# RWKV-7 chunk stage: the block inverses of both head halves taken level by level in turn, ahead of all sums

## The chip, the cores and the metric

The kernel runs on one core of one Trainium2 chip. The metric is the device time of one execution in microseconds (us). Engines are named as in the profile: PE is TensorE's matmul side, PEld its weight loads, DVE is VectorE, ACT is ScalarE, POOL is GpSimd, SP is SyncE, which issues loads. Everything is float32; a float32 product shows as two PE records.

## The reference, cut to what matters

Two decoder layers are computed for 1,040 prompt tokens (16 meta tokens and 1,024 others) and for 8 samples of 4 tokens. Layer 0 mixes with latent attention, layer 1 with RWKV-7 time mixing, and each is followed by a squared-ReLU MLP. The change touches RWKV-7 alone, which has 16 heads of 64 and, by token,

```python
def _wkv_step(S, inp):
    r, w, k, v, a, b = inp
    sa = jnp.einsum('bhvk,bhk->bhv', S, a)
    S = S * w[:, :, None, :] + sa[..., None] * b[:, :, None, :] + v[..., None] * k[:, :, None, :]
    return S, jnp.einsum('bhvk,bhk->bhv', S, r)
```

Then `y` is normalized by head, scaled by `ln_w`, shifted by `ln_b`, gets the term `(sum(r*k*r_k)) * v`, is multiplied by a gate and goes through `w_o`.

## The kernel before

**Chunks.** The recurrence is done in chunks of 128 tokens: chunks 0 to 7 in `chunk(c, ...)`, and a tail of 48 tokens behind them. Chunks 1 to 6 run in a hardware loop of three turns with two chunks each. Inside a chunk the state solves a triangular system for each head, so a 128x128 unit triangular matrix is inverted by head. Heads are done in two halves of eight, d = 0 and d = 1.

**The inverse.** `low_inverses(c)` on DVE inverts the 16x16 diagonal blocks of all 16 heads of a chunk and signals `low_b` at its last transpose (line 2899). It needs `diagonals(c)` on ACT (line 2141), which copies the blocks out of the masked products `MA`, and those are made by `before_keys(c)` on PE and masked on DVE (line 2800). The larger blocks come from three levels, each a pair of dependent products with a copy behind each: `level_16` (spread block X4 from ACT line 2178, W4 masked on DVE line 2831, sum in `blocks_32`, lines 2836 and 2838, signalled by `e32_b`), `level_32` (X5 and XT spread by ACT line 2178, W5 by line 2197, XT by line 2203) and `level_64` (turned block, XW6 by ACT lines 1835 and 2211, XT by line 2215). X4, X5, W5 and XT each exist once, so the second half can begin only after the first is through.

**The sums.** `b_with_r`, `k_with_both` make products that DVE masks (line 2800). `first_sums(d)` gives P1; `finals(d)` multiplies P1 by the inverse, whose copy is `SA` (ACT line 1835), makes the change of the state (read by DVE's `new_half(d)`, lines 2946 and 2734) and the outputs Y.

**Preparing chunk c+1 inside chunk c.** Its path is: `key_sums` (PE), `clamp` (DVE line 2738), `norms` (ACT line 2124), `inverse_norms` (DVE line 2760), `key_scales` (PE), `normed_keys` (DVE line 2766); `rates` (PE), `both_rates` (ACT line 2109), `sums` (DVE lines 2751 to 2755, signals `cum_b`); `sums_before` (POOL line 1739), `decays_before` (ACT line 2134), `a_keys` (DVE line 2772), `b_keys` (DVE lines 2734 and 2782, signals `b_b`), `before_keys` (PE), `k_keys` (DVE), `diagonals` and `low_inverses`.

**Finishing chunk c-1 inside chunk c.** `centre` (DVE), `squares` (ACT line 2229), `variances` (DVE), `deviations` (ACT line 2233), `scale_outputs` (DVE lines 2923 and 2925, signals `scaled_b`), `group_norm` on POOL (lines 1744, 1746, 1748), `gates` (PE), `gated` (DVE line 2933), `turn_z` (PE), `z_to_store` (ACT).

**Order.** There is no planner. Each engine's `chunk` is a list written out by hand and each engine works through its own list in order; semaphores (`Beat.wait`) hold an engine until another has signalled. Two rings of four PSUM banks each lie between PE and ACT (`ra`) and between PE and DVE (`rv`). `keep_busy` is a product of 256 columns that nobody reads; a chunk has nine of them. POOL's list, which the change leaves alone, is:

```python
if prepare: scale_keys(c + 1, wn)
if finish:  y_b.wait(pool, c - 1); bonus_terms(c - 1, ...)
if finish:  group_norm(c - 1, P, Y[1 - par], vt[1 - par])   # waits scaled_b
if prepare: sums_before(c + 1, wn)                           # waits cum_b
...
if prepare: decay_r(c + 1, ...); bonus(c + 1, wn)
if finish:  store_z(c - 1)
```

`finish` is false in chunk 0 alone. PE's list before is b_with_r(0), k_with_both(0), level_16(0), level_32(0), level_64(0), finals(0), then b_with_r(1), k_with_both(1), level_16(1), before_keys(c+1), level_32(1), level_64(1), finals(1), with other work as fillers between the two products of each level.

Of the kernel before, what the change touches and what calls it, by code (L numbers as in the profile page):

```python
# [18 lines left out]
P = 128  # L19
# [141 lines left out]
def program(nc, A, O):  # L161
    ctx = ExitStack()
    with ctx:
# [180 lines left out]
        X4, X5, W5 = q(512), q(1024), q(1024)  # L344
# [10 lines left out]
        W4 = hx[:, 7168:8192]  # L355
# [25 lines left out]
        values_4 = [X5, W5]  # L381
# [80 lines left out]
        def _(pe):  # L462
# [532 lines left out]
            def turn_b_k(c, w):  # L995

                bk_b.wait(pe, c)
                for src in (Bt, Kt):
# [87 lines left out]
            def level_16(c, d, ma, filler):  # L1086
# [3 lines left out]
                for j in range(8):  # L1090
                    for rows, cols in diagonal(8 * d + j):
                        ins = mm(b[rows, j * 64:(j + 1) * 64], ma[rows, cols], X4[rows, j * 64:(j + 1) * 64], True, True)
                rv.done(ins)
                w4_at = rv.filled.n
                filler()
                if d == 1:
                    keep_busy(rv)
                b = narrow(rv, w4_at)
# [6 lines left out]
            def level_32(c, d, ma, filler):  # L1105
# [7 lines left out]
                w5_at = ra.filled.n  # L1113
                filler()
                xt_b.wait(pe, c, d + 1)
                keep_busy(ra)
                b = narrow(ra, w5_at)
                for j in range(8):
                    for rows, cols in diagonal(j):
                        ins = mm(b[rows, j * 64:(j + 1) * 64], W5[rows, j * 64:(j + 1) * 64], XT[rows, cols], True, True)  # L1120
                ra.done(ins)

            def level_64(d, ma, fillers):

                crossed_at = ra.filled.n
                fillers[2]()
                keep_busy(ra)
                b = narrow(ra, crossed_at)
                for j in range(8):
                    ins = turn(b[0:64, j * 64:(j + 1) * 64], XT[0:64, j * P:j * P + 64], 64)  # L1130
                ra.done(ins)
                turned_at = ra.filled.n
                fillers[0]()
                keep_busy(ra)
                b = narrow(ra, turned_at)
# [4 lines left out]
                w6_at = ra.filled.n  # L1140
                fillers[1]()
                b = narrow(ra, w6_at)
                for j in range(8):
                    ins = mm(b[0:64, j * 64:(j + 1) * 64], XW6[64:P, j * 64:(j + 1) * 64], XT[64:P, j * P + 64:(j + 1) * P], True, True)
                ra.done(ins)

            def chunk(c, par, nth, finish=True, prepare=True, wn=P):
# [15 lines left out]
                def finals(d, taken, stated):  # L1163
# [4 lines left out]
                    for j in range(8):  # L1168
                        ins = mm(b[:, j * RN:(j + 1) * RN], XT[:, j * P:(j + 1) * P],
# [45 lines left out]
                level_16(c, 1, ma, nothing)  # L1215
# [610 lines left out]
        def _(act):  # L1826
# [333 lines left out]
            def tokens(w):  # L2160
                for dst in (Btok, Ktok):
# [19 lines left out]
            def spread_16(c, d):  # L2181

                low_b.wait(act, c)
                if not isinstance(c, int) or c > 0 or d > 0:
                    e32_b.wait(act, c, d)
                signal(quadrants(X4, 64, XE[:, d * 256:(d + 1) * 256]), x4_b)

            def spread_32(c, d):

                e32_b.wait(act, c, d + 1)  # L2190
                signal(quadrants(X5[:, 0:512], 64, XE32), x5_b)
                signal(quadrants(XT, P, XD32), xt_b)

            def take_w_32():
                b = ring.bank()
                for rows in (32, 96):
                    ins = act.copy(heads(W5[:, 0:512], 64)[rows:rows + 32, :, 0:32], heads(b[:, :], 64)[rows:rows + 32, :, 0:32])
                lane.do(ins, ring.drained)

            def take_x_32():  # L2200
                b = ring.bank()
                for rows in (0, 64):
                    ins = act.copy(heads(XT, P)[rows:rows + 32, :, rows + 32:rows + 64], heads(b[:, :], 64)[rows:rows + 32, :, 32:64])
# [9 lines left out]
            def take_x_64():  # L2213
                b = ring.bank()
                lane.do(act.copy(heads(XT, P)[0:64, :, 64:P], heads(b[:, :], 64)[0:64, :, :]), ring.drained)
# [30 lines left out]
            def chunk(c, par, finish=True, prepare=True, wn=P):  # L2246
                if prepare:
                    lora_columns(c + 1, wn)
                tokens(P)
                spread_32(c, 0)  # L2250
                take_w_32()
                bonus_out(P)
                if prepare:
                    square_keys(c + 1, wn)
                take_x_32()
                bonus_factors(par, P)
                if finish:
# [12 lines left out]
                spread_16(c, 1)  # L2270
# [6 lines left out]

# [895 lines left out]
```

How the kernel before makes its waits and increments, by code:

```python
    def bank(self, free=False, ahead=0):  # L110
        n = self.filled.n + ahead
        if n >= len(self.banks) and not free:
            self.eng.wait_ge(self.drained, self.filled.value(len(self.banks) - 1 - ahead))
        return self.banks[n % len(self.banks)]
# [4 lines left out]
    def wait_drained(self, back=0):  # L120
        self.eng.wait_ge(self.drained, self.filled.value(back))
# [8 lines left out]
    def wait(self, eng, chunk, n=None):  # L131
        eng.wait_ge(self.sem, chunk * self.per + (self.per if n is None else n))
# [8 lines left out]
    def bank(self):  # L141
        self.eng.wait_ge(self.filled, self.drained.value(-1))
        return self.banks[self.drained.n % len(self.banks)]
# [12 lines left out]
    def settle(self):  # L157
        self.eng.wait_ge(self.last.sem, self.last.value())
# [289 lines left out]
        def meet(eng, here):  # L448
            here.add(eng.drain())
            here.n += 4
            eng.wait_ge(meet_s, here.n)
# [19 lines left out]
            def apart(semaphore, value):  # L472
                pe.wait_ge(semaphore, value)
                pe.sem_inc(narrow_s, 1)
# [4 lines left out]
            def norm(scratch, n):  # L480
                for at, w in PIECES:
                    sq_t.expect()
                    pe.wait_ge(sq_s, sq_t.n)
                    b = ra.bank()
                    for k in range(n):
                        ins = mm(b[:, 0:w], ones, scratch[:, k, at:at + w], k == 0, k == n - 1)
                    ra.done(ins)
# [1 line left out]
            def sums_at(layer, p, ks, b):  # L490
                w = PIECES[p][1]
                sq_t.expect()
                pe.wait_ge(sq_s, sq_t.n)
                for k in ks:
```

## Time and profile before

| what | value |
|---|---|
| three runs | 3689.3, 3693.97, 3695.07 us; median 3693.97 |
| profiled execution | 3694.62 us; span of its records 3692.9 us |
| PE busy in the span | 3481.3 us, 94% |
| DVE, ACT, POOL busy | 47%, 26%, 16% |
| mean granted TensorE clock | 0.959 of full |
| chunk stage (first to ninth `low_inverses`) | 2086.6 to 2676.4 us |

The profile gives one execution. The chunk stage is a sixth of it. The granted clock is the share of TensorE's full clock of 2.4 GHz that the chip allowed; it has two levels, 1.0 and 0.5 (2.4 and 1.2 GHz). A row of the timeline is: start in us, duration in us, engine, line, operation, output<-input, size, count, and in brackets how long the engine was idle before it and who ended that.

### The profile page before, as it was taken

What the parts mean: (1) busy time and instruction counts of PE and PEld (TensorE: products, weight loads), DVE (VectorE), ACT (ScalarE), POOL (GpSimd) and SP (SyncE); (2) the same over time, 40 slices, a digit from 0 to 9 for tenths busy, and PEclk for the clock granted to TensorE, in tenths of its full rate; (3) what the DMA queues carried; (4) which work ended last, traced back from release to release, by engine and by line L of the source; (5) the groups of instructions that cost most, each with busy time, mean ns of one, the idle gap of its engine ahead of it and who ended that gap; (6) DMA issues with size and microseconds to landing.
All of it is one profiled execution on the core that took longest, in us unless ns stands there. A gap on an engine that the chain in (4) does not pass through costs nothing.

```text
span 3692.9 us, 62858 instructions
## 1 busy us (share of the span) xinstructions
PE 3481.3 (94%) x24636; PEld 3069.2 (83%) x24636; DVE 1734.6 (47%) x3220; ACT 976.3 (26%) x1832; POOL 582.1 (16%) x241
## 2 busy tenths in 40 slices
PE   9999998999999999998999788888899999999998
PEld 6667666756999999996899677777785799999998
DVE  3545454214544444446203367667631644444445
ACT  2223333511111111112214255556520211111111
POOL 0000000000211212211222122223220122221111
PEclk9999998999999999999999889999969999999999
DMA  3222121510111111102222101000151111111101
GB/s 101 55 75 59 41 71 44 198 56 34 46 45 45 45 45 45 45 1 93 83 71 102 65 13 41 30 25 24 31 171 35 57 46 45 45 45 45 45 29 48
DMA packets 151723, 207.26 MB, mean 56 GB/s; under 512 B 42670, under 2 KB 126689, under 8 KB 151170
## 3 DMA queue, kind: packets, MB, share of 16 engines
q1 hardware_dynamic: 145506, 185.08, 15.2%
q0 software_dynamic: 6048, 19.73, 1.6%
q8 instruction: 130, 2.13, 0.2%
q14 instruction: 39, 0.32, 0.0%
HBM read 174.39 MB, written 50.82 MB: 61 GB/s over the span
## 4 chain that ended last, share of the span: by engine, by line
PE 66%; PEld 6%; DVE 5%; issue 3%; ACT 1%; DMA 1%; SPq 0%; DVEq 0%; ACTq 0%; PEldq 0%; POOLq 0%; POOL 0%
PE bank L470 64%; PEld bank L470 6%; PE bank L478 2%; DVE hT L2800 1%; DVE arena L2734 1%; DVE arena L2635 1%; SPq L1399 0%; ACT arena L2178 0%; DMA arena<-in_rwkv_a_w 0%; DVE n_lo L2602 0%; DVE arena L2751 0%; DMA arena<-arena 0%; ACT arena L1835 0%; DVE arena L2782 0%; DVE arena L2766 0%
## 5 line engine op out<-in xcount | busy, mean ns | idle before, releaser
L470 PE MATMUL bank<-arena 128*32 128x128 f32 (+15 forms) x8142 | 1174.2, 340 | 95.6 <-DVE hT L2800 26.5
L470 PEld LDWEIGHTS bank<-arena 128*128 128x128 f32 (+7 forms) x8142 | 837.5, 180 | 410.2 <-issue 122.1
L2433 DVE TENSOR_TENSOR hT<-hT,bank 128x384 f32<-128x384 f32 (+1 forms) x816 | 425.7, 526 | 501.9 <-PE bank L470 501.5
L470 PE MATMUL bank<-u_hi,dn_hi 128*128 128x384 f32 (+1 forms) x1536 | 494.9, 326 | 12.9 <-DVE hT L2433 8.3
L470 PE MATMUL bank<-u_lo,dn_hi 128*128 128x384 f32 (+1 forms) x1536 | 496.1, 327 | 0.0
L470 PE MATMUL bank<-n_hi,up_hi 128*128 128x384 f32 (+1 forms) x1536 | 489.6, 325 | 2.2 <-ACT arena L2019 2.2
L470 PE MATMUL bank<-n_lo,up_hi 128*128 128x384 f32 (+1 forms) x1536 | 489.5, 325 | 0.0
L1835 ACT COPY arena<-bank 128x512 f32<-128x512 f32 (+15 forms) x573 | 261.2, 491 | 856.5 <-PE bank L470 598.8
L1672 POOL TENSOR_TENSOR up_lo<-arena,up_hi 128x2048 fp32r<-128x2048 f32 x32 | 148.0, 4624 | 1559.9 <-ACT up_hi L2003 1559.9
L470 PE MATMUL bank<-u_hi,dn_lo 128*128 128x384 f32 (+1 forms) x1536 | 375.2, 326 | 0.0
L2635 DVE TENSOR_TENSOR arena<-arena 128x384 f32<-128x384 f32 (+1 forms) x192 | 163.9, 854 | 435.4 <-ACT arena L2019 435.4
L470 PEld LDWEIGHTS bank<-u_hi,dn_hi 128*128 128x128 f32 x1536 | 289.4, 188 | 15.4 <-DVE hT L2433 8.9
L470 PEld LDWEIGHTS bank<-n_hi,up_hi 128*128 128x128 f32 x1536 | 289.5, 188 | 2.9 <-ACT arena L2019 2.5
L470 PEld LDWEIGHTS bank<-u_lo,dn_hi 128*128 128x128 f32 x1536 | 289.8, 189 | 0.3
L470 PEld LDWEIGHTS bank<-n_lo,up_hi 128*128 128x128 f32 x1536 | 289.3, 188 | 0.1
L470 PE MATMUL bank<-n_hi,up_lo 128*128 128x384 f32 (+1 forms) x1536 | 282.4, 325 | 1.2 <-POOL up_lo L1672 1.2
L470 PEld LDWEIGHTS bank<-u_hi,dn_lo 128*128 128x128 f32 x1536 | 271.6, 189 | 0.0
L470 PEld LDWEIGHTS bank<-n_hi,up_lo 128*128 128x128 f32 x1536 | 256.1, 188 | 1.5 <-POOL up_lo L1672 1.5
L2019 ACT ACTIVATE arena<-bank 128x384 f32<-128x384 f32 (+1 forms) x192 | 89.6, 469 | 591.3 <-PE bank L470 584.2
L1672 POOL TENSOR_TENSOR dn_lo<-arena,dn_hi 128x2048 fp32r<-128x2048 f32 x32 | 147.4, 4606 | 617.5 <-ACT dn_hi L2009 617.5
L2009 ACT ACTIVATE dn_hi<-arena 128x2048 fp32r<-128x2048 f32 x32 | 61.4, 1920 | 649.9 <-PE bank L470 643.9
L470 PE MATMUL bank<-arena,hT 64*64 64x64 f32 (+3 forms) x2432 | 170.5, 255 | 47.1 <-ACT arena L2178 25.8
(207 smaller groups left out, 3948.6 us busy)
## 6 DMA issues: line engine op xcount, KB each, us to landing
arena<-in_ffn_w_up SPq DMA_DIRECT2D x32, 1024.0 KB, 5.6
arena<-in_ffn_w_down SPq DMA_DIRECT2D x32, 1024.0 KB, 7.7
arena<-past_scratch SPq DMA_DIRECT2D x32, 640.0 KB, 8.1
past_scratch<-in_cache_kv_latent SPq DMA_DIRECT2D x128, 128.0 KB, 2.4
hidden_scratch<-hT SPq DMA_DIRECT2D x1, 4288.0 KB, 13.1
past_scratch<-in_cache_k_rope SPq DMA_DIRECT2D x128, 32.0 KB, 2.1
arena<-in_rwkv_w_r SPq DMA_DIRECT2D x4, 1024.0 KB, 8.0
r_scratch<-arena POOLq DMA_DIRECT2D x8, 512.0 KB, 5.7
```

The lines of the kernel that those rows point to most:

```text
L470: return pe.matmul(out, lhsT, rhs, start=first, stop=last, skip_group_check=group)
L478: return pe.transpose(out, src, ident[0:rows, 0:rows])
L1672: lo_t.add(pool.tensor_tensor(lo[:, :, :], raw[:, :, :], hi[:, :, :].bitcast(F32), ALU.subtract))
L1835: lane.do(act.copy(dst, b if view is None else view(b)), ring.drained)
L2009: lane.do(act.activation(dn_hi[:, :, :], w_dn[par][:, :, :], ACT.Copy), hi_t)
L2019: lane.do(act.activation(relu[(u_t.n - 1) % 4][:, 0:w], b[:, 0:w], ACT.Relu), ring.drained)
L2433: lane.do(dve.tensor_tensor(hT[:, k, at:at + w], hT[:, k, at:at + w], b[:, 0:w], ALU.add), ring.drained)
L2635: lane.do(dve.tensor_tensor(r, r, r, ALU.mult))
L2734: lane.do(dve.tensor_tensor(out, a, b, op))
L2800: lane.do(dve.tensor_tensor(dst.rearrange("p (h z w) -> p h z w", h=heads, z=2)[:, :, z, :], b[:, 0:heads * n].rearrange("p (h w) -> p h w ...
```

## The change

X4 and XT get a second buffer each (X4 one by half, `XTs` one by half), each of the three level functions is cut into its first and second product, and PE's list in a chunk becomes: the levels of both halves step by step in turn, then the sums of half 0, then the sums of half 1, with `before_keys(c+1)` and `gates` and `turn_z` around the sums of half 1. ACT and DVE take their copies and masks in the matching order, and some other steps change places in their lists (`scale_outputs` behind `sums`, `norms` and `deviations` behind the SA copy, `diagonals` behind the second SA copy, both `spread_16` at the chunk's end). Nine `keep_busy` stay in a chunk; six of them now lie between the level steps. Four memsets at the stage's start become six (X4 twice, XT twice).

```diff
             def chunk(c, par, nth, finish=True, prepare=True, wn=P):    # PE
+                level_16_first(c, 0, ma)
                 r_b.wait(pe, c)
                 b_with_r(0, ar)
+                level_16_second(0)
+                level_16_first(c, 1, ma)
                 bk_b.wait(pe, c)
                 k_with_both(0, 0, ar)
                 k_with_both(0, 1, ar)
-                level_16(c, 0, ma, lambda: turn_b_k(c, P))
-                level_32(c, 0, ma, lambda: bonus_sums(c, P))
-                bonus_at = ra.filled.n - 1
+                level_16_second(1)
+                keep_busy(ra)
+                level_32_first(c, 0, ma)
+                turn_b_k(c, P, (Bt,))
+                keep_busy(ra)
+                level_32_second(c, 0)
+                bonus_sums(c, P)
+                bonus_at = ra.filled.n
+                level_32_first(c, 1, ma)
+                turn_b_k(c, P, (Kt,))
+                level_64_turned(0)
+                level_32_second(c, 1)
+                keep_busy(rv)
+                level_64_first(0, ma)
+                keep_busy(rv)
+                level_64_turned(1)
+                keep_busy(rv)
+                level_64_second(0)
+                keep_busy(rv)
+                level_64_first(1, ma)
                 v_in[par].wait(pe, nth)
-                level_64(0, ma, [when(prepare, lambda: key_sums(c + 1, wn)), lambda: first_sums(0), lambda: turn_bonus(P, bonus_at)])
+                first_sums(0)
+                if prepare:
+                    key_sums(c + 1, wn)
+                level_64_second(1)
+                turn_bonus(P, bonus_at)
                 finals(0, when(prepare, lambda: rates(c + 1, wn, 0)), when(prepare, lambda: (rates(c + 1, wn, 1), key_scales(c + 1, wn))))
 
                 b_with_r(1, ar)
                 k_with_both(1, 0, ar)
                 k_with_both(1, 1, ar)
-                level_16(c, 1, ma, nothing)
+                keep_busy(ra)
+                rv.wait_drained()
+                first_sums(1)
                 if wn == TAIL:
                     before_keys_tail(AR[1 - par])
                 elif prepare:
                     before_keys(c + 1, AR[1 - par])
-                level_32(c, 1, ma, when(finish, lambda: gates(c - 1, P)))
-                level_64(1, ma, [nothing, lambda: first_sums(1), nothing])
-                finals(1, when(finish, lambda: turn_z(c - 1, P, Y[1 - par])), nothing)
+                finals(1, when(finish, lambda: gates(c - 1, P)), nothing)
+                if finish:
+                    turn_z(c - 1, P, Y[1 - par])
...
             def chunk(c, par, finish=True, prepare=True, wn=P):         # ACT
                 if prepare:
                     lora_columns(c + 1, wn)
-                tokens(P)
                 spread_32(c, 0)
+                spread_turned(0)
                 take_w_32()
+                tokens(P, (Btok,))
+                spread_32(c, 1)
+                take_x_32(0)
                 bonus_out(P)
+                spread_turned(1)
+                take_w_32()
+                tokens(P, (Ktok,))
+                take_turned()
+                take_x_32(1)
+                take_w_64()
+                take_turned()
+                take_x_64(0)
+                take_w_64()
                 if prepare:
                     square_keys(c + 1, wn)
-                take_x_32()
-                bonus_factors(par, P)
+                take(P1, P, 512)
+                take_x_64(1)
                 if finish:
                     squares(c - 1, P, Y[1 - par])
-                take_turned()
-                take_w_64()
+                bonus_factors(par, P)
+                take(SA, P, 512)
                 if prepare:
                     norms(c + 1, wn)
+                    both_rates(c + 1, wn)
                 if finish:
                     deviations(c - 1, P)
-                take(P1, P, 512)
-                take_x_64()
-                take(SA, P, 512)
-                if prepare:
-                    both_rates(c + 1, wn)
-                spread_16(c, 1)
                 if prepare:
                     decays(c + 1, wn, wn == TAIL)
                 take(Y[par][:, 0:512], P, 512)
                 if prepare:
                     decays_before(c + 1, wn)
                     key_factors(c + 1, wn)
-
-                spread_32(c, 1)
-                take_w_32()
+                take(P1, P, 512)
+                take(SA, P, 512)
                 if wn == TAIL:
                     diagonals_tail()
                 elif prepare:
                     diagonals(c + 1, MA[1 - par])
...
                     spread_16(c + 1, 0)
+                    spread_16(c + 1, 1)
...
             def chunk(c, par, finish=True, prepare=True, wn=P):         # DVE
+                if finish:
+
+                    y_b.wait(dve, c - 1)
+                level_16(0)
                 b_with_r()
+                blocks_32(c, 0)
+                level_16(1)
                 k_with_both(0)
                 k_with_both(1)
-                if finish:
-
-                    y_b.wait(dve, c - 1)
-                level_16(0)
+                blocks_32(c, 1)
                 scale_state()
-                blocks_32(c, 0)
...
-                if finish:
-                    scale_outputs(c - 1, P, Y[1 - par])
                 new_half(0)
                 if prepare:
                     normed_keys(c + 1, wn)
                     sums(c + 1, wn, wn == TAIL)
+                if finish:
+                    scale_outputs(c - 1, P, Y[1 - par])
 
                 b_with_r()
                 k_with_both(0)
                 k_with_both(1)
                 if prepare:
                     a_keys(c + 1, 1 - par, wn)
-                level_16(1)
-                if prepare:
                     b_keys(c + 1, wn)
-                blocks_32(c, 1)
```

## Rows read from the trace of the kernel before

**Rows 1.** Windows: span, PE, PEld, DVE, ACT, POOL busy (count), clock, DMA share, GB/s.

```profile
2086.60:2676.40 589.80, 510.88 (x5932) 440.82 (x5933) 396.85 (x681) 332.77 (x733) 147.79 (x74) 0.90 0.09 26
2310.00:2387.50 77.50, 65.85 (x751) 56.10 (x751) 52.22 (x88) 42.87 (x93) 20.33 (x11) 0.89 0.09 27
```

**Rows 2.** Line 2899, end of `low_inverses`: count, duration min/median/max ns, first and last start.

```profile
L2899 DVE STREAM_TRANSPOSE arena<-arena x9: 995/1065/1079, 2085.6 to 2675.3; 128x512 f32<-128x512 f32 x9
```

**Rows 3.** Timeline of PE in one chunk, 2314 to 2391 us.

```profile
2314.53 2.95 PE L470 MATMUL bank<-arena 64*128 64x128 f32 x24 [1.54 <-issue]
2320.44 1.97 PE L470 MATMUL bank<-arena,hT 64*64 64x64 f32 x32
...
2328.38 1.37 PE L470 MATMUL bank<-arena,hT 64*64 64x64 f32 x32 [3.02 <-ACT arena L2178]
...
2357.83 1.15 PE L470 MATMUL bank<-arena,hT 64*64 64x64 f32 x32
2358.91 0.70 PE L470 MATMUL bank<-table 128*128 128x256 f32 x2
2362.11 1.12 PE L470 MATMUL bank<-arena,hT 64*64 64x32 f32 x32 [2.50 <-DVE hT L2831]
2364.68 3.79 PE L470 MATMUL bank<-arena 64*128 64x128 f32 x32 [1.45 <-DVE arena L2782]
```

**Rows 4.** Timeline of DVE in the same chunk, the path to the next chunk's keys.

```profile
2340.85 1.23 DVE L2925 TENSOR_TENSOR arena<-arena 128x1024 f32<-128x1024 f32 x1
2347.14 0.69 DVE L2946 TENSOR_TENSOR arena<-bank,table 128x512 f32<-128x512 f32 x1 [5.07 <-PE bank L470]
2347.87 2.78 DVE L2734 TENSOR_TENSOR arena<-arena 128x512 f32<-128x512 f32 x2
2350.56 1.28 DVE L2766 TENSOR_TENSOR arena<-arena,bank 128x512 f32<-128x512 f32 x2
2351.76 2.29 DVE L2751 TENSOR_TENSOR_SCAN arena<-arena 128x1024 f32<-128x1024 f32 x1
...
2354.28 1.23 DVE L2755 TENSOR_TENSOR arena<-arena 128x1024 f32<-128x1024 f32 x1
...
2359.33 2.03 DVE L2772 SCALAR_TENSOR_TENSOR arena<-arena 128x1024 f32<-128x1024 f32 x1
```

**Rows 5.** Timeline of DVE, first and last rows of `low_inverses`, two chunks.

```profile
2074.84 1.04 DVE L2852 STREAM_TRANSPOSE arena<-arena 128x512 f32<-128x512 f32 x1 [2.69 <-ACTq L2143]
...
2085.61 0.99 DVE L2899 STREAM_TRANSPOSE arena<-arena 128x512 f32<-128x512 f32 x1
...
2373.80 1.05 DVE L2852 STREAM_TRANSPOSE arena<-arena 128x512 f32<-128x512 f32 x1
...
2386.39 1.06 DVE L2899 STREAM_TRANSPOSE arena<-arena 128x512 f32<-128x512 f32 x1
```

**Rows 6.** Timeline of POOL in the same chunk, `group_norm`'s first step and `sums_before`.

```profile
2342.15 2.35 POOL L1744 TENSOR_TENSOR arena<-arena 128x1024 f32<-128x1024 f32 x1 [26.52 <-DVE arena L2925]
...
2355.59 2.37 POOL L1739 TENSOR_TENSOR arena<-arena 128x1024 f32<-128x1024 f32 x1 [6.22 <-DVE arena L2755]
```

**Rows 7.** Timeline of ACT in the same chunk.

```profile
2326.34 3.31 ACT L2178 COPY arena<-arena 32x256 f32<-32x256 f32 x8 [1.25 <-DVE arena L2838]
...
2338.11 1.28 ACT L2124 ACT_TABLE_LOAD   x1
2339.40 0.31 ACT L2124 ACTIVATE arena<-arena 128x128 f32<-128x128 f32 x1
...
2344.07 0.59 ACT L1835 COPY arena<-bank 128x512 f32<-128x512 f32 x1 [2.09 <-PE bank L470]
...
2358.02 1.06 ACT L2134 ACTIVATE arena<-arena 128x1024 f32<-128x1024 f32 x1
...
2371.12 2.50 ACT L2141 COPY arena<-hT 32x512 f32<-32x512 f32 x4
```

**Rows 8.** Timeline of DVE, first masks of the tail.

```profile
2683.44 2.98 DVE L2813 TENSOR_TENSOR hT<-bank,arena 48x384 f32<-48x384 f32 x6 [3.11 <-PE bank L470]
```

More of the change, by code:

```diff
@@ L343, in program @@
         zbuf = q(8, P)
-        X4, X5, W5 = q(512), q(1024), q(1024)
+        values_at = q.at
+        X4a, X5, W5, XT_b = q(512), q(512), q(512), q(1024)
         XD, XW6, XD32 = q(512), q(512), q(256)
@@ L993, in _, with turn_b_k @@
             mark["chunks_a"], mark["chunks_v"] = ra.filled.n, rv.filled.n
-            def turn_b_k(c, w):
+            def turn_b_k(c, w, sources=(Bt, Kt)):
                 bk_b.wait(pe, c)
-                for src in (Bt, Kt):
+                for src in sources:
                     for half in range(2):
@@ L1084, in diagonal, with level_16_first @@
                 return [(slice(z * 64, (z + 1) * 64), slice(h * P + z * 64, h * P + (z + 1) * 64)) for z in range(2)]
-            def level_16(c, d, ma, filler):
+            drained_at = {}
+            def level_16_first(c, d, ma):
                 apart(x4_b.sem, c * x4_b.per + d + 1)
@@ L1091, in level_16, with level_16_second @@
                     for rows, cols in diagonal(8 * d + j):
-                        ins = mm(b[rows, j * 64:(j + 1) * 64], ma[rows, cols], X4[rows, j * 64:(j + 1) * 64], True, True)
+                        ins = mm(b[rows, j * 64:(j + 1) * 64], ma[rows, cols], X4[d][rows, j * 64:(j + 1) * 64], True, True)
                 rv.done(ins)
[L1094 to L1098, printed above, removed]
+                drained_at["w4", d] = rv.filled.n
+            def level_16_second(d):
+                b = narrow(rv, drained_at["w4", d])
                 for j in range(8):
@@ L1103, in level_16, with level_32_first @@
                 rv.done(ins)
-            def level_32(c, d, ma, filler):
+            def level_32_first(c, d, ma):
                 apart(x5_b.sem, c * x5_b.per + d + 1)
@@ L2158, in spread_tail, with tokens @@
                 act.drain().then_inc(xt_tail_s, 1)
-            def tokens(w):
-                for dst in (Btok, Ktok):
+            def tokens(w, dsts=(Btok, Ktok)):
+                for dst in dsts:
                     for half in range(2):
@@ L2183, in spread_16, with spread_turned @@
                 low_b.wait(act, c)
-                if not isinstance(c, int) or c > 0 or d > 0:
-                    e32_b.wait(act, c, d)
-                signal(quadrants(X4, 64, XE[:, d * 256:(d + 1) * 256]), x4_b)
+                signal(quadrants(X4[d], 64, XE[:, d * 256:(d + 1) * 256]), x4_b)
             def spread_32(c, d):
                 e32_b.wait(act, c, d + 1)
-                signal(quadrants(X5[:, 0:512], 64, XE32), x5_b)
-                signal(quadrants(XT, P, XD32), xt_b)
+                signal(quadrants(X5, 64, XE32), x5_b)
+            def spread_turned(d):
+                signal(quadrants(XTs[d], P, XD32), xt_b)
             def take_w_32():
@@ L2196, in take_w_32, with take_x_32 @@
                 for rows in (32, 96):
-                    ins = act.copy(heads(W5[:, 0:512], 64)[rows:rows + 32, :, 0:32], heads(b[:, :], 64)[rows:rows + 32, :, 0:32])
+                    ins = act.copy(heads(W5, 64)[rows:rows + 32, :, 0:32], heads(b[:, :], 64)[rows:rows + 32, :, 0:32])
                 lane.do(ins, ring.drained)
-            def take_x_32():
+            def take_x_32(d):
                 b = ring.bank()
                 for rows in (0, 64):
-                    ins = act.copy(heads(XT, P)[rows:rows + 32, :, rows + 32:rows + 64], heads(b[:, :], 64)[rows:rows + 32, :, 32:64])
+                    ins = act.copy(heads(XTs[d], P)[rows:rows + 32, :, rows + 32:rows + 64], heads(b[:, :], 64)[rows:rows + 32, :, 32:64])
                 lane.do(ins, ring.drained)
@@ L2211, in take_w_64, with take_x_64 @@
                 lane.do(act.copy(XW6[64:P, :], b[64:P, :]), ring.drained)
-            def take_x_64():
+            def take_x_64(d):
                 b = ring.bank()
-                lane.do(act.copy(heads(XT, P)[0:64, :, 64:P], heads(b[:, :], 64)[0:64, :, :]), ring.drained)
+                lane.do(act.copy(heads(XTs[d], P)[0:64, :, 64:P], heads(b[:, :], 64)[0:64, :, :]), ring.drained)
             def key_factors(c, w):
@@ L2283, in chunk @@
                     diagonals(c + 1, MA[1 - par])
-                take_x_32()
-                take_turned()
-                take_w_64()
-                take(P1, P, 512)
-                take_x_64()
-                take(SA, P, 512)
+                take(Y[par][:, 512:1024], P, 512)
+                signal(act.drain(), y_b)
                 if finish:
                     z_to_store(c - 1)
-                take(Y[par][:, 512:1024], P, 512)
-                signal(act.drain(), y_b)
                 if wn == TAIL:
@@ L2830, in level_16 @@
                 b = ring.bank()
-                lane.do(dve.tensor_tensor(heads(W4[:, 0:512], 64), heads(b[:, :], 64),
+                lane.do(dve.tensor_tensor(heads(W4, 64), heads(b[:, :], 64),
                                           mix("siblings_16").unsqueeze(1).broadcast_to([P, 8, 64]), ALU.mult), ring.drained)
             def blocks_32(c, d):
+                if d == 1:
+                    xt_b.wait(dve, c, 1)
                 b = ring.bank()
@@ L3018, in _ @@
             lane.settle()
-            for t in (X4, X5[:, 0:512], W5[:, 0:512], XT):
+            for t in (*X4, X5, W5, *XTs):
                 lane.do(dve.memset(t, 0.0))
```

48 lines of the change are left out of this document (23 added, 25 removed).

## The prediction

> **What bounds the kernel now.** I read the page first: PE is busy in most of the span, but the change touches only the chunk stage. So I looked at windows next. From the end of the first `low_inverses` to the end of the ninth the span is 589.8 us and PE is busy for 510.9 [rows 1]: 78.9 us idle, 9.9 us a chunk, and the granted clock is 0.90, so about a fifth of the stage runs at its lower level of 1.2 GHz. The nine ends of `low_inverses` lie 589.7 us apart over eight chunks, 73.7 us each [rows 2]. The chunk shown below took 77.4 us (2310.0 to 2387.45).
>
> Then the timeline of PE says what the idle time is [rows 3]: 3.02 us before `level_32` of half 0, until ACT has spread the blocks; 2.50 us before the second product of `level_16` of half 1, until DVE has masked W4; 1.45 us before `before_keys`, until DVE has made the B keys; and smaller ones. After the 3.02 and the 2.50 us of idle the clock falls: 32 records of 64x64 take 1.97 us at the lower level and 1.15 us at the upper one. So the levels do cost something. The question is what the other engines' lists do.
>
> The reader should see a second chain, which runs from chunk to chunk. It begins where the copy of SA for half 0 ends, at 2344.07 + 0.59 = 2344.66; call this moment t. It goes through DVE, POOL, ACT and PE to `before_keys` and `low_inverses`, whose end at 2387.45 is t + 42.8 [rows 4, 5, 7]. Before the change it is nearly hidden: PE waits only 1.45 us for its B keys, since level and state work of half 1 lies beside it, and between `before_keys` (2364.68) and the next chunk's first use of the low inverse PE has 30 us of work. The chain is to be costed again in the new order.
>
> **The change, part by part.** A chunk is cut in two stretches: from the end of `low_inverses` (call it T) to t, and from t to the next T. Before, the first is 2344.66 - 2310.0 = 34.6 us.
>
> *From T to t, the ladder.* The next chunk's first product is now `level_16_first(0)`, which needs the low inverse, so nothing covers it any more: spreading is half of the 3.31 us that eight such copies take [rows 7], 1.65 us, and with about 0.4 us to PE's start it is 2.05. Behind that I take the old stretch from the chunk's first product to t (2344.66 - 2314.53 = 30.1 us) and correct it. The level products of half 1 move in: seven steps, six of them of about 1.12 us and one of transposes at half of that, about 7.4 us [rows 3]. Six unread products instead of three: 3 x about 0.6 = 1.8 us (a pair takes 0.70 and overlaps its neighbour [rows 3]). The level waits of half 0 go: 3.02 us and four of under 1 us, 4.8 us. New waits come, about 2.5 us: half 1's XT is spread on ACT behind half 0's copies, which delays W5 of half 1 by about 0.9; and `finals(0)` needs all of its ring drained, whose last bank is now read by `bonus_factors` behind `squares`, about 1.7. Sum 30.1 + 7.4 + 1.8 - 4.8 + 2.5 = 37.0; with 2.05, T to t is 39.0 us against 34.6. The steps as such save little: the chain in one half is filled with the other half's steps, but the work is now all ahead of t. Bounds: every wait gone and the upper clock throughout gives 33.5 + 2 = 35.5; 1.5 us more of copies on ACT gives 40.5.
>
> *From t to the next T.* Step by step, in us after t:
> - `norms` is now behind the SA copy on ACT: load of its table 1.28 and 0.31 [rows 7], 1.65. The reciprocal on DVE, 0.95, ends at 2.65.
> - `new_half(0)`: 0.69, then two passes, 2.78 beside POOL [rows 4], about 2.1 where POOL is idle, as it now is: 5.5. `normed_keys` 1.28: 6.75. `sums`, from 2351.76 to 2354.28 + 1.23 in the rows [rows 4], 3.75: `cum_b` at 10.45. (`both_rates` gives its input at 6.4, just in time.)
> - `scale_outputs` now stands behind `sums`: 0.2 and 1.23 [rows 4]: 11.9. Before, it had ended at 2342.1, ahead of t.
> - POOL's list is unchanged: `group_norm` stands ahead of `sums_before`. `group_norm` was released by `scale_outputs` at 2342.15 and had 6.2 us to spare before `cum_b` released `sums_before` at 2355.59 [rows 6]. Now it begins only at 11.9, three passes of 2.35 with their gaps 7.2: 19.2. Then `sums_before` 2.37: 21.6. This puts the normalization of chunk c-1 into the path of chunk c+1. It is the largest term.
> - `decays_before` on ACT 1.06 [rows 7]: 22.75. `a_keys` on DVE about 1.95 [rows 4]: 24.7. `b_keys`, two passes of 1.23 [rows 4]: 27.2. Before, these ended at 2364.6, t + 19.9, although DVE also masked W4 on the way. The masks of half 1 (six of 0.69) fill DVE's wait.
> - `before_keys`: PE has been idle since about 19.5 and so is at the lower clock, 3.79 us [rows 3], and its last mask ends 5.2 after its start, as it did: 32.5. PE is through at 31.1.
> - `diagonals` on ACT is now behind the second SA copy, and that one behind P1's product, which stands behind `before_keys`: unread product 0.7 to 1.2, P1 product 2 to 3, copy 0.6: 35.0. `diagonals` 2.50 [rows 7]: 37.6.
> - `low_inverses`: 13.65 in the chunk shown, 11.8 in the first one, where POOL ran nothing beside it [rows 5]. POOL's `bonus` now ends about 2 us into it; I take 12.3. The next T is at t + 50.0, against 42.8 in this chunk.
>
> A full chunk is 39.0 + 50.0 = 89.0 us. PE's cover behind `before_keys` is now `finals(1)` with `gates` and `turn_z`, about 12 us, and the next product needs the low inverse, 21 us after `before_keys` has ended; so PE idles some 9 us there and 8 us ahead of `before_keys`, and begins after both at the lower clock, which is in the figures.
>
> Chunk 0 finishes no chunk: no `group_norm`, `squares` and table switch in the path, 39.0 - 1.4 and 39.6 (the masks end at t + 13.4, the B keys at 17.9): 77.2. Chunk 7 prepares the tail of 48 columns, so `sums_before`, keys and `diagonals` are short: 39 + 42 = 81. Eight chunks: 77.2 + 6 x 89.0 + 81 = 692.2, against 589.7 [rows 2]: +102.5. The second buffers' two memsets ahead of the first `low_inverses`: +1.3. The tail's masks began at 2683.44 [rows 8], 7.0 after the last T, held by PE's `finals(1)`; that is now through by then, and only `new_half(1)` lies between, 2.8: -4.2. Sum +99.6, on the profiled execution's own 3694.6 us: 3794.2. That execution is within 0.7 us of the median. Nothing behind the stage is timed by anything but it, so all of it is passed on.
>
> **Table loads.** The load ahead of `norms` starts at 2338.11, lasts 1.28, and the function starts at 2339.40 [rows 7]; the new order has one more switch a chunk, as `norms` and `deviations` no longer share one, and I price a switch at 1.28. The Trainium skill ("ScalarE: Activation LUTs", What ACT_TABLE_LOAD costs) gives about 2.66 us for a switch, the load and a drain of about 1.38. This trace shows the load and no drain beside it. With the drain, an estimate from that page, the two switches ahead of `sums` would put 1.4 to 2.8 us more on seven chunks and the result at 3804 to 3814.
>
> **The rivals.**
> - *The levels' waits are what counts and the rest stays hidden.* For it: 5.5 us of level waits a chunk and the lower clock behind them. Those 5.5 us and about 3 us of lower clock would go, 8 x 8.5 = 68 us less: 3626. Against it: PE's cover behind `before_keys` shrinks from 30 us to 12. It decides if `low_inverses` ends within 12 us of `before_keys`, which its own 11.8 us and `diagonals` exclude unless `before_keys` moves ahead by 9. Chance 0.06.
> - *The B keys are not held by POOL.* If `group_norm` ends before `cum_b` can matter (`scaled_b` early, or POOL's passes fast), the B keys come when DVE has done its masks: 11.9 + 3.8 + 1.95 + 2.5 = 20.2 instead of 27.2, seven times 7 us less: 3745. Chance 0.11.
> - *The copies on ACT bind the ladder, or table switches are dearer*: 5 us more a chunk, 3834. ACT then has a copy behind each of twelve products, in one list. Chance 0.07.
> - *Gain and loss cancel*: the change leaves the time within its noise. Both stretches would have to be 7 us shorter each. Chance 0.02.
>
> **How the numbers follow.** My forecast, the chain through `group_norm`, has 0.74. Its own range: low ends are 3.5 us less in the ladder and 2.5 less after t (upper clock in `before_keys` and P1's product), eight times 6, 3746; high ends 1.5 and 2.5 more, 3826. The range 3744 to 3828 takes in that and the second rival's centre, and leaves out less than 2 in 10. Differences under 0.2% (7 us) can't be told from none here. Faster by more: 0.06; within: 0.02; slower: 0.92.
>
> **What would show it.** Right: `sums_before` (POOL, line 1739) starting directly behind line 1748 instead of behind DVE line 2755; line 2925 behind line 2755; PE idle 7 to 9 us twice a chunk, once until DVE line 2782 (`before_keys`), once until ACT line 2178 (`level_16_first`), with the clock at its lower level behind both; line 2899 at intervals of about 89 us; `low_inverses` shorter than 13 us; no idle over 1 us between level steps. Wrong if PE's wait for line 2782 is under 3 us, if the intervals are under 82 us, or if the ladder from the X4 copy to SA takes over 41 us: then a copy on ACT is late, and the rows of lines 2197 to 2215 would show it.

## The result, and the profile after

The changed kernel takes 3801.5 us (median of 4 runs, 3793.2 to 3803.3) against 3692.9 us: ratio 1.0291, 95% interval 1.0277 to 1.0305, or +109 us. The forecast was 3794, range 3744 to 3828, and slower. The profiled execution took 3802.4 us. One execution below, a fourth of experiment 3, fell in the chip's slower state (4036.1 us at a mean granted clock of 0.82) and is left out of the comparison.

Line numbers move by 2 to 36: lines 2800, 2831, 2925, 2755, 2772, 2782 and 2899 of before are 2834, 2865, 2961, 2789, 2806, 2816 and 2935; POOL's 1739 and 1744 are 1771 and 1776; ACT's 1835, 2178 and 2134 are 1867, 2210 and 2166.

The ends of `low_inverses`, as in [rows 2]:

```profile
L2935 DVE STREAM_TRANSPOSE arena<-arena x9: 993/996/1009, 2084.9 to 2783.7; 128x512 f32<-128x512 f32 x9
```

From the first of these ends to the ninth it is 698.8 us instead of 589.7, so +109.1: all of the difference lies in this stage. The eight intervals are 77.4, 89.8, 86.8, 93.4, 89.5, 89.0, 89.9 and 83.1 us. The six in the middle, called full chunks below, average 89.7; before the change they were 79.5, 73.0, 77.4, 73.9, 73.9 and 73.6, on average 75.2.

One chunk by windows (columns as in [rows 1]); its end of `low_inverses` is at 2339.90, its t at 2378.54, the next end at 2433.29:

```profile
2345.00:2349.40 4.40, 4.40 (x74) 4.14 (x72) 2.15 (x4) 0.62 (x2) 0.00 (x0) 0.50 0.00 0
2349.40:2378.50 29.10, 26.57 (x371) 21.91 (x369) 9.17 (x14) 17.81 (x40) 0.00 (x0) 0.97 0.01 2
2378.50:2397.70 19.20, 17.28 (x158) 15.38 (x156) 12.89 (x17) 12.82 (x27) 6.42 (x3) 0.92 0.00 1
2397.70:2406.60 8.90, 0.00 (x0) 0.00 (x0) 4.72 (x3) 4.60 (x10) 5.23 (x3) 0.74 0.00 0
2406.60:2412.50 5.90, 5.84 (x41) 5.44 (x42) 3.18 (x5) 0.00 (x0) 0.00 (x0) 0.52 0.00 0
2412.50:2422.50 10.00, 10.00 (x81) 9.22 (x80) 8.59 (x31) 3.53 (x6) 4.28 (x2) 1.00 0.41 136
2422.50:2435.30 12.80, 0.04 (x1) 0.00 (x0) 12.48 (x13) 2.99 (x7) 4.66 (x3) 0.63 0.19 59
2435.30:2440.00 4.70, 4.64 (x70) 4.33 (x70) 1.33 (x3) 1.60 (x5) 0.00 (x0) 0.55 0.00 0
```

Read the PE column: through the ladder (second row) PE is busy 26.6 of 29.1 us, so the change does what it was built to do. Then there are two holes without any product, 8.9 and 12.8 us, and behind each the clock is at 0.50 to 0.55. The two rows of PE that end the holes, against [rows 3]:

```profile
2406.66 3.79 PE L472 MATMUL bank<-arena 64*128 64x128 f32 x32 [8.97 <-DVE arena L2816]
...
2435.36 1.97 PE L472 MATMUL bank<-arena,hT 64*64 64x64 f32 x32 [12.81 <-ACT arena L2210]
```

The first is `before_keys` waiting for the B keys (1.45 us before the change), the second `level_16_first(0)` waiting for the spread low inverse (no such wait before). All six full chunks have both: 8.97 to 8.99 us, and 10.6 to 12.9. DVE's rows on the way, against [rows 4, 5]:

```profile
2388.39 1.22 DVE L2789 TENSOR_TENSOR arena<-arena 128x1024 f32<-128x1024 f32 x1
...
2389.81 1.23 DVE L2961 TENSOR_TENSOR arena<-arena 128x1024 f32<-128x1024 f32 x1
2390.96 3.79 DVE L2834 TENSOR_TENSOR hT<-bank,arena 128x512 f32<-128x512 f32 x6
2401.75 2.27 DVE L2806 SCALAR_TENSOR_TENSOR arena<-arena 128x1024 f32<-128x1024 f32 x1 [7.00 <-ACT arena L2166]
...
2424.85 5.07 DVE L2919 TENSOR_TENSOR arena<-arena 128x512 f32<-128x512 f32 x1
...
2432.30 0.99 DVE L2935 STREAM_TRANSPOSE arena<-arena 128x512 f32<-128x512 f32 x1
```

And POOL's, against [rows 6]:

```profile
2391.12 2.36 POOL L1776 TENSOR_TENSOR arena<-arena 128x1024 f32<-128x1024 f32 x1 [51.40 <-DVE arena L2961]
2393.56 2.35 POOL L1778 TENSOR_TENSOR arena<-arena 128x1024 f32<-128x1024 f32 x1
2395.99 2.34 POOL L1780 TENSOR_TENSOR arena<-arena 128x1024 f32<-128x1024 f32 x1
2398.29 2.34 POOL L1771 TENSOR_TENSOR arena<-arena 128x1024 f32<-128x1024 f32 x1
...
2425.16 1.97 POOL L1747 TENSOR_TENSOR arena<-arena,prm 128x1024 f32<-128x1024 f32 x1
2427.03 1.95 POOL L1765 TENSOR_TENSOR std<-std,arena 128x1024 f32<-128x1024 f32 x1
```

`sums_before` (line 1771) stands directly behind `group_norm`, although `cum_b` was there at 2389.6, 8.7 us earlier. DVE masks what it has (2834) and idles for 7.0 us until ACT's `decays_before`, which follows POOL. The B keys end at 2406.54, t + 28.0. The last two rows are `scale_keys` and `bonus_terms` of the next chunk's list; DVE's long product (line 2919, 5.07 us) lies beside them, inside `low_inverses`.

### The profile page after: what moved, and what is told of

Read it like the earlier page. It is cut to its first block, busy times and chain, and to the rows that moved or that the text cites. A ratio compares the mean times of both kernels' runs of the same rounds, so it can differ in the third digit from the quotient of the medians.

```text
span 3800.6 us, 62843 instructions
## 1 busy us (share of the span) xinstructions
PE 3464.0 (91%) x24636; PEld 3060.2 (81%) x24636; DVE 1744.4 (46%) x3222; ACT 983.2 (26%) x1839; POOL 584.2 (15%) x241
## 4 chain that ended last, share of the span: by engine, by line
PE 58%; issue 10%; PEld 6%; DVE 4%; POOL 2%; ACT 1%; DMA 1%; SPq 0%; DVEq 0%; ACTq 0%; PEldq 0%; POOLq 0%
PE bank L472 56%; PEld bank L472 6%; PE bank L480 2%; DVE arena L2669 1%; SPq L1431 0%; POOL arena L1776 0%; POOL arena L1778 0%; DVE arena L2806 0%; POOL arena L1780 0%; POOL arena L1771 0%; DMA arena<-in_rwkv_a_w 0%; DVE n_lo L2636 0%; DMA arena<-arena 0%; DVE arena L2919 0%; DVE arena L2768 0%
## 5 line engine op out<-in xcount | busy, mean ns | idle before, releaser
L472 PE MATMUL bank<-arena 128*32 128x128 f32 (+16 forms) x8142 | 1165.4, 338 | 160.4 <-DVE arena L2816 58.6
L472 PE MATMUL bank<-u_hi,dn_hi 128*128 128x384 f32 (+1 forms) x1536 | 496.3, 327 | 12.9 <-DVE hT L2467 8.3
L1867 ACT COPY arena<-bank 128x512 f32<-128x512 f32 (+14 forms) x573 | 261.4, 489 | 845.8 <-PE bank L472 623.2
L472 PE MATMUL bank<-arena,hT 64*64 64x64 f32 (+3 forms) x2176 | 149.4, 246 | 113.5 <-ACT arena L2210 113.4
L472 PEld LDWEIGHTS bank<-arena,hT 64*64 64x64 f32 (+2 forms) x2176 | 136.5, 161 | 130.1 <-issue 129.7
```

What stands on the lines that cost most here:

```text
L472: return pe.matmul(out, lhsT, rhs, start=first, stop=last, skip_group_check=group)
L1867: lane.do(act.copy(dst, b if view is None else view(b)), ring.drained)
```

## The experiments

Each experiment ran on one chip together with runs of the kernel before, and its ratio is to those; microseconds against the changed kernel compare across chips (the medians of the kernel before lie between 3691.4 and 3693.4 us everywhere). `t` and `T` are as in the prediction.

**1. POOL's order exchanged.**

```diff
+                if prepare:
+                    sums_before(c + 1, wn)
                 if finish:
                     group_norm(c - 1, P, Y[1 - par], vt[1 - par])
-                if prepare:
-                    sums_before(c + 1, wn)
```

> The changed kernel with one pair exchanged in POOL's list: sums_before(c+1) ahead of group_norm(c-1). Theory (group_norm holds the B keys): a_keys then waits for cum_b + 2.4 + 1.1 = t + 14.6 or for the masks of half 1 (t + 16.2), whichever is later, so the B keys come at t + 20.8 instead of t + 28.0; 7 us in each of the 7 chunks that finish one: 3801.5 - 49 = 3752. Rival (the low inverses' new place at the head of PE's list is the bound, and the B keys are early enough): no change, 3801. Line 1771 should start directly behind line 2789.

Measured 3790.6 us, 1.0261 (1.0237 to 1.0285). Line 1771 did start behind 2789, but only some 11 us were won, where the theory had 49. The intervals of this ratio and the changed kernel's overlap, so the time does not exclude the rival's "no change"; the trace gives another reason than the rival's. It shows where the gain went. DVE and POOL in that kernel:

```profile
2389.64 3.32 DVE L2961 TENSOR_TENSOR arena<-arena 128x1024 f32<-128x1024 f32 x1
2392.88 2.47 DVE L2834 TENSOR_TENSOR hT<-bank,arena 128x512 f32<-128x512 f32 x4
...
2398.98 3.26 DVE L2768 TENSOR_TENSOR arena<-arena 128x1024 f32<-128x1024 f32 x1
2402.28 3.25 DVE L2816 TENSOR_TENSOR arena<-arena 128x1024 f32<-128x1024 f32 x1
```

```profile
2389.53 2.35 POOL L1771 TENSOR_TENSOR arena<-arena 128x1024 f32<-128x1024 f32 x1 [50.70 <-DVE arena L2789]
...
2397.90 3.25 POOL L1780 TENSOR_TENSOR arena<-arena 128x1024 f32<-128x1024 f32 x1
2401.12 3.32 POOL L1752 TENSOR_TENSOR arena<-arena 128x1024 f32<-128x1024 f32 x1
```

Passes of DVE that take 1.23 us take 3.3 beside a POOL pass, and POOL's own grow to 3.3. `scale_outputs` and both passes of `b_keys` together lose 6.1 us, of 7.2 that the exchange frees. So the wait for `group_norm` became a slowdown by `group_norm`.

**2. `scale_outputs` and `deviations` back at their places** (DVE: ahead of `new_half(0)`; ACT: `deviations` beside `norms`, ahead of `both_rates`).

> The changed kernel with scale_outputs back ahead of new_half(0) on DVE and deviations back beside norms on ACT (one table switch less); POOL's list as changed. Theory: group_norm runs from t + 4.2 to t + 11.4, new_half and with it cum_b move from t + 11.1 to about t + 12.5, sums_before ends at 14.9, the B keys come at t + 20.5: 7.5 us less in 7 chunks, 3749. Rival (late new_half costs what POOL gives): within 10 us of 3801.

Measured 3779.2 us, 1.026 (1.0189 to 1.0331): the interval is too wide for a size (the four runs lie between 3762.7 and 3818.4). Its profile shows line 2816 end at t + 24.0 instead of t + 28.0, not at 20.5: `group_norm` now runs beside `new_half` and the scan of `sums`.

```profile
2376.24 4.93 DVE L2768 TENSOR_TENSOR arena<-arena 128x512 f32<-128x512 f32 x2
...
2382.29 3.25 DVE L2785 TENSOR_TENSOR_SCAN arena<-arena 128x1024 f32<-128x1024 f32 x1
```

The two products of `new_half` take 4.93 instead of 1.42 us and the scan 3.25 instead of 2.28.

**3. That move alone, in the kernel before.**

```diff
-                if finish:
-                    scale_outputs(c - 1, P, Y[1 - par])
                 new_half(0)
                 if prepare:
                     normed_keys(c + 1, wn)
                     sums(c + 1, wn, wn == TAIL)
+                if finish:
+                    scale_outputs(c - 1, P, Y[1 - par])
```

> The kernel before with that one move alone: scale_outputs behind sums on DVE. Theory: group_norm then ends about t + 19.5, the B keys come at t + 27.5 instead of t + 19.9, and PE's wait of 1.45 us ahead of before_keys and its wait for W4 of half 1 grow by 7.5 us in sum, 7 chunks: 3692.9 + 52 = 3745. Rival (the kernel before has work of half 1 to cover it): under 3705.

Measured 3733.2, 3735.5 and 3745.4 us, 1.013 (1.0100 to 1.0161): by the ratio +48 us (+37 to +59), near the 52 expected. Its list of waits between 2160 and 2700 us (who waited for whom, us in total, times, longest) shows the chain:

```profile
PE bank L470 <- DVE hT L2831: 62.4, 7, 9.6
ACT arena L2134 <- POOL arena L1739: 56.9, 7, 8.4
DVE arena L2772 <- ACT arena L2134: 44.8, 7, 7.0
```

PE's longest wait for W4 (line 2831) grows from 2.5 us [rows 3] to 9.6. Moving one operation of 1.2 us behind `sums` is enough for nearly half of the change's loss. In the full chunks the stretch from t to T is 50.0 us on average, where the kernel before has 42.7 and the changed one 53.0.

**4. `group_norm` cut to 8 of 1,024 columns**, in the changed kernel and in the one before. The kernel leaves scale, shift and bonus out of the other columns.

```diff
-                lane.do(pool.tensor_tensor(out[0:w, :], out[0:w, :], lnw[0:w, :], ALU.mult))
+                lane.do(pool.tensor_tensor(out[0:w, 0:8], out[0:w, 0:8], lnw[0:w, 0:8], ALU.mult))
...
```

> The changed kernel with group_norm's three POOL passes cut from 1,024 to 8 columns (the outputs of chunks lack their scale, shift and bonus). This takes away the wait and the contention together. Theory (group_norm in the key path costs its 7.2 us): B keys at t + 21.2 instead of t + 28.0, 6.8 us in 7 chunks: 3801.5 - 48 = 3753. Rival (B keys are not what times the chunk, as the exchange in POOL's list seemed to say): 3790 as there.

> The same cut in the kernel before. Theory (its group_norm is hidden, but stretches the two passes of line 2734 by 0.7 us a chunk): 3693 - 5 = 3688. Rival (group_norm costs its time there too): 3640 to 3650.

Measured 3746.7 us, 1.0147 (1.0126 to 1.0168), and 3678.7 us, 0.9969 (0.9957 to 0.9981). The first theory holds to 6 us; PE's waits for the B keys fall from 53.9 to 15.3 us over six chunks. In the kernel before, the cut gives 13 instead of 5 us: even a hidden `group_norm` has a price. Without it the change costs 1.0147 / 0.9969 = 1.018, some 66 us; `group_norm` is the other 43 or so of 109. By the traces the 66 us are the longer `low_inverses`, which now stand uncovered, and the longer stretch from T to t.

**5. `low_inverses`' last step left out**, in both: the blocks of 16 are then inverted by blocks of 8 only.

```diff
-                for size in (4, 8):
+                for size in (4,):
```

> The changed kernel with low_inverses' last step left out (two products and two sums of line 2919 and 2924, so blocks of 16 stay inverted only in blocks of 8): 3.5 us of DVE and, where POOL holds the second product up, 3 to 4 more. Theory (low_inverses are uncovered at each chunk's start): 3.5 us in 8 chunks and some of the contention, 3801.5 - 28 to -45: 3757 to 3773. Rival (PE's idle time there is only what POOL's wait has moved): no change.

> The same step left out of the kernel before. Theory (low_inverses end some 5 to 7 us before PE comes for them, so they are covered): 0 to 5 us less, 3688 to 3693. Rival (they are on the path in both): 28 us less, 3665.

Measured 3761.4 us, 1.0184 (1.0161 to 1.0207), and 3685.6 us, 0.9983 (0.9971 to 0.9996): 40 us less in the changed kernel, 6 in the one before. The first is within what the theory expected, the second 1 us beyond its 0 to 5. Between 2160 and 2700 us PE's longest wait for the spread inverse falls from 13.2 us in the changed kernel to 5.4 in its shortened form:

```profile
PE bank L472 <- ACT arena L2210: 37.5, 13, 5.4
```

The same DVE work is on the path in one order and nearly off it in the other.

**6. POOL kept away from `low_inverses`**: `scale_keys` and `bonus_terms` wait for `low_b` of their chunk.

```diff
+                low_b.wait(pool, c)
                 if prepare:
                     scale_keys(c + 1, wn)
```

> The changed kernel with POOL's scale_keys and bonus_terms held until low_b of their chunk, so that they no longer run beside low_inverses. Theory (the long line 2919 of 4.1 to 5.1 us in 5 of 9 low_inverses is DVE starved by two POOL passes back to back): it falls to 1.1 us everywhere, 3 to 4 us less in five chunks and 1 in a sixth, 3801.5 - 18 = 3784. Rival (the long row is the record's, not the engine's, or the POOL work is then late for square_keys): no change or slower.

Measured 3787.0 us, 1.0266 (1.0244 to 1.0289). The groups of line 2919 (2920 there) between 2086 and 2780 us, in the changed kernel and then in this one:

```profile
L2919 DVE TENSOR_TENSOR arena<-arena 128x512 f32<-128x512 f32 x16 | 34.5, 2156 | 0.6
```

```profile
L2920 DVE TENSOR_TENSOR arena<-arena 128x512 f32<-128x512 f32 x16 | 16.8, 1050 | 0.6
```

17.7 us of DVE time go, as expected, and the time is 15 us lower; the two ratios' intervals overlap, so the rows show the cause and the time only agrees. In the full chunks `low_inverses` fall from 16.0 to 13.0 us on average and the stretch from t to T from 53.0 to 50.2.

**7. `b_with_r(0)` ahead of `level_16_first(0)`**, on PE and DVE.

> The changed kernel with b_with_r(0) ahead of level_16_first(0) on PE and DVE, so that PE has 2 us of work while it waits for the low inverse. Theory: about 1.5 to 2 us a chunk after the first, 3801.5 - 12 = 3790. Rival (DVE's masks of it then delay W4 by as much): no change.

Measured 3809.5 us, 1.0314 (1.0297 to 1.0332): if anything 8 us slower, where the theory had 12 us faster. A full chunk is 92.1 us. The stretch from T to t is 37.4 us against 36.7, not shorter: DVE masks R's products ahead of W4, so PE waits 0.88 us there, and the granted clock of the stretch is 0.86 or 0.87, where five of the changed kernel's six full chunks have 0.91 to 0.93. And line 2919 takes 4.9 to 5.0 us in five of the six, where the changed kernel has one at 1.08 and the others at 4.1 to 5.1. Why POOL meets it so evenly is open.

**8. The six unread products left out.**

> The changed kernel without the six unread products between the level steps. Theory (the steps of two halves cover most of each other's copies, so a product of 0.6 us costs about 0.4): 8 chunks x 2.5 = 20 us less, 3781. Rival (they hold the clock up through the ladder): the clock falls to 0.5 in the ladder and the time is 3801 or above.

Measured 3818.7 us, 1.0338 (1.0321 to 1.0355): 17 us slower. Windows of one chunk's ladder and what follows it, in this kernel:

```profile
2450.00:2458.00 8.00, 6.02 (x112) 5.38 (x113) 1.08 (x1) 7.11 (x18) 0.00 (x0) 1.00 0.01 2
2458.00:2472.00 14.00, 13.38 (x95) 11.89 (x92) 1.51 (x2) 4.59 (x8) 0.00 (x0) 0.51 0.00 1
```

and in the changed kernel:

```profile
2359.00:2367.00 8.00, 7.50 (x114) 5.92 (x114) 0.00 (x0) 6.18 (x15) 0.00 (x0) 1.00 0.00 0
2367.00:2381.00 14.00, 12.81 (x130) 11.32 (x129) 2.32 (x3) 7.60 (x12) 0.00 (x0) 0.90 0.01 2
```

With gaps of 0.2 to 1.3 us between the level steps, PE is busy 6.0 of 8 us and the clock then falls to 1.2 GHz for 14 us. This is so in four of the six full chunks, where T to t rose to 40 us (granted clock 0.71). In one with the same gaps the clock held (0.91) and T to t was 33.5 us, against 36.2 in the changed kernel: the theory's 2.5 us are there and are lost to the clock. The rival was right. It is not the whole loss: over the full chunks T to t grew by 1.5 us on average and t to T by 2.1, there with a lower clock too (mostly 0.78 against 0.79 to 0.84) and with line 2919 at 5.0 to 5.3 us in five chunks.

**9. All that seemed to help, together.**

```diff
# PE
+                r_b.wait(pe, c)
+                b_with_r(0, ar)
                 level_16_first(c, 0, ma)
...
                 first_sums(1)
+                if finish:
+                    gates(c - 1, P)
# ACT
                 take(P1, P, 512)
+                diagonals(c + 1, MA[1 - par])
                 take(SA, P, 512)
# DVE
                     b_keys(c + 1, wn)
+                if finish:
+                    gated(c - 1, P, Y[1 - par])
```

and the edits of experiments 2 and 6.

> The changed kernel with all that seems to help: scale_outputs and deviations back at their places, POOL's scale_keys and bonus_terms held until low_b, b_with_r(0) ahead, diagonals ahead of the second SA copy, gates and gated ahead of before_keys. Theory: 24 of 28 us to the B keys, 2.5 less before low_inverses, 3 less inside them, 1.5 at the start: the chunk falls from 89.7 to about 79, 3693 + 8 x 5.5 = 3737. Rival (the new order of the levels would beat the old one if the rest did not stand in its way): under 3693.

Measured 3782.8 us, 1.0253 (1.0232 to 1.0275): neither; only 19 of 64 us. PE's rows at the start of a chunk and ahead of `k_with_both(1)`:

```profile
2422.32 1.97 PE L472 MATMUL bank<-arena,hT 64*64 64x64 f32 x32 [5.73 <-ACT arena L2213]
2427.44 1.92 PE L472 MATMUL bank<-arena,hT 64*64 64x32 f32 x32 [3.15 <-DVE hT L2868]
...
2477.67 2.08 PE L472 MATMUL bank<-arena 64*128 64x256 f32 x8 [4.70 <-DVE hT L2837]
```

and DVE's beside the first of them:

```profile
2420.84 4.36 DVE L2771 TENSOR_TENSOR arena<-arena 128x512 f32<-128x512 f32 x2
```

The wait for the spread inverse is down to 5.7 us, but POOL's held work now meets `new_half(1)` (4.36 us instead of 1.42), which delays R's masks and W4 by 3 us, and `group_norm` still meets `new_half(0)` (5.10 us at 2465.49). So in the full chunks t to T falls from 53.0 to 47.7 us on average, and T to t rises from 36.7 to 40.3.

**10. One idea of the change in the kernel before.**

```diff
                 r_b.wait(pe, c)
                 b_with_r(0, ar)
-                bk_b.wait(pe, c)
-                k_with_both(0, 0, ar)
-                k_with_both(0, 1, ar)
-                level_16(c, 0, ma, lambda: turn_b_k(c, P))
+                level_16(c, 0, ma, keys)    # bk_b.wait and both k_with_both
+                turn_b_k(c, P)
```

with DVE's masks in that order and ACT spreading X5 ahead of the B and K rows.

> The kernel before with one idea of the change and no more, for half 0: the first product of level_16 ahead of k_with_both, which then lies between its two products, and the turning of the B and K rows behind them, beside ACT's spreading of X5 (spread ahead of the copies of the turned rows). Half 1's levels, the keys and the normalization stay. Theory: the 3.0 us wait ahead of level_32 is filled with 2 us of turning, a new wait of about 1.3 us for X4 opens, and a shorter lower-clock stretch gives 1 us; 1.7 us a chunk, 3692 - 14 = 3678, below both kernels. Rival (X4 comes as late as it was needed, because ACT spreads it behind the Y copy, and the rest is order only): no change, 3692, or slower.

Measured 3694.5 us, 1.0007 (0.9992 to 1.0021): no change, as the rival said. Its reason, a late X4, is not what the rows show: `level_16`'s first product follows at once (2311.03). The 3.0 us wait was split, not filled:

```profile
2320.34 1.15 PE L470 MATMUL bank<-arena,hT 64*64 64x64 f32 x32 [1.87 <-ACT arena L1838]
...
2323.46 0.69 PE L470 MATMUL bank<-table 128*128 128x256 f32 x2 [1.40 <-ACT arena L2181]
```

PE now waits for ACT's copies of the rows it has turned (a free bank), and then for XT, which ACT spreads behind them. No version that beats the kernel before was found.

## Why the prediction was right

*Where the time goes.* Right, in both places and with both releasers. The normalization of chunk c-1 in the key path was called the largest term; experiments 3 and 4 confirm it from two sides (+48 us by that move alone; 43 of 109 by leaving the work out). The low inverse at the head of the chunk is the other; experiment 5 shows it.

*T to t.* Predicted 39.0. The six full chunks average 36.7, the one shown 38.6. The ladder itself was costed rightly: the first product starts 2.07 us after T (2.05 laid out), and behind it PE is idle for 0.84, 0.50 and 1.19 us in every full chunk, 2.5 in sum, which is what was laid out for new waits. What was off is the stretch that the sum starts from. It was taken from one chunk of the kernel before, 34.6 us at a granted clock of 0.85; the six full ones took 36.7, 30.2, 34.6, 31.5, 31.1 and 30.9, on average 32.5. In the changed kernel too the 38.6 us go with a clock of 0.85, and the five others (36.1 to 36.7) with 0.91 to 0.93 and the same waits. From the average, the same sum gives 36.9.

*t to T.* Predicted 50.0; the average is 89.7 - 36.7 = 53.0, the chunk shown 54.75. B keys at t + 28.0 against 27.2: right. Behind them the steps are as laid out except `low_inverses`, priced at 12.3 us and measured from 2416.76 to 2433.29, 16.5. This is the term that was mis-sized. The prediction let POOL's `bonus` touch its first 2 us, but `scale_keys` and `bonus_terms` of the next chunk also run there, since nothing in POOL's list holds them until the low inverse is ready. (Nor was the first chunk's 11.8 us quite free of POOL: a pass of POOL, 2074.04 to 2075.95, lay beside its first 1.1 us.) Experiment 6 holds them back: line 2919 gets 17.7 us shorter over the stage, and the average from t to T is then 50.2 us.

*The two signs that failed.* `low_inverses` were to be shorter than 13 us and took 16.5. PE's second idle stretch was to be 7 to 9 us and was 12.81, longer by about what `low_inverses` were. The other signs came: line 1771 directly behind line 1780, line 2961 behind 2789, the first idle stretch 8.97 us, the clock at its lower level behind both, no idle over 1 us between level steps.

*The sum.* The two errors, about -2.3 and +3 us a chunk, cancel by luck. Chunk 0 (77.2 predicted, 77.4 measured) and chunk 7 (81 and 83.1) are near. Eight chunks were to take 692.2 us and took 698.8. Outside them, the memsets' +1.3 us is not seen: the first `low_inverses` end 0.7 us earlier than before. The tail gain of 4.2 us is not left in the total: its masks do begin at 2786.88, 2.1 behind T instead of 7.0, but the stage's end moved by 108.3 (from 2676.4 to 2784.7) and the span's end by 107.7. So nearly all that was gained there was given back behind it; where is open.

*What no experiment isolates.* Over the six full chunks the loss is 14.5 us each. From t to T it is 10.3: 7.3 come with the place of `scale_outputs` alone (experiment 3, 42.7 to 50.0), and the other 3 are about what experiment 6 takes back. The 4.2 us from T to t (32.5 to 36.7) are read from the traces; no run takes that step alone.

*Table loads.* Each load is 1.28 or 1.29 us, and where nothing else holds ACT the function follows within 0.02 us in the changed kernel too. The Trainium skill ("ScalarE: Activation LUTs", What ACT_TABLE_LOAD costs) has a drain of about 1.38 us as well; it does not show here. In the chunk shown `cum_b` came at t + 11.1, 0.6 us later than laid out, since `new_half(0)` waited 1.47 us for PE's product; `sums` did not wait for ACT.

*The rivals.* The second (B keys not held by POOL) was priced at 7 us a chunk if `group_norm` were out of the way. That size is right when the work is left out (6.8 expected, 7.5 found: 89.7 to 82.2 for a full chunk), and wrong when it is only moved (experiment 1: 1 us), because it then slows DVE. The third (copies on ACT bind the ladder) is not seen: no wait in the ladder is over 1.2 us. The first and the fourth would need a time that is lower or the same.

## What to carry to other kernels

Filling the waits of a dependent ladder with its twin's steps works, and is worthless if it takes the work away that covered a longer chain on another engine; cost that chain, engine by engine and in each one's list order, before moving anything. When an operation moves on one engine, look up what the others have queued behind its signal: here a product of 1.2 us on VectorE moved 7 us of GpSimd work into the path. Moving GpSimd work out of a path gave less here than priced where it came to lie beside VectorE passes between two SBUF operands (experiments 1, 2 and 9). And take the starting figure of a sum from the average of all chunks: the one chunk that this prediction started from was 2 us longer than the average.

## What the runs showed of the hardware

A VectorE pass over 128x1024 with both operands in SBUF took 1.23 us alone and 3.3 us when GpSimd ran a pass beside it, and GpSimd's own grew from 2.35 to as much. By the ends of the rows the two engines take turns, a whole pass each: in experiment 1, in all six full chunks, VectorE's passes of lines 2768 and 2816 end 1.08 to 1.09 us behind the end of the GpSimd pass that started before them, and GpSimd's pass of line 1752 ends 2.19 to 2.20 us behind the VectorE pass that started before it.

A product of 128x512 took 1.02 to 1.10 us alone and up to 5.07 in the changed kernel. There it waited for two GpSimd passes (2425.16 to 2428.98), of which the second starts before the first has ended, and ended 0.94 us behind the second. Why VectorE gets no turn between these two, and gets one between lines 1780 and 1752 of experiment 1, is open.

VectorE's masks, whose first operand is in PSUM, are not slowed: four took 2.48 us with GpSimd idle (changed kernel, 2351.27) and 2.47 beside its passes (experiment 1, 2392.88).
